# A two-layer decoder trunk on one Trainium2 core: value products moved behind the next round's scores, and the first expert quad's first two weight slots cut by k block

## The reference

```
h = rms_norm(x);  z = h @ w_in + b_in          # 8448 columns: A q/k/v, B u/v, C q/k/v, three gates
A: 16 heads of 64, 4 key/value heads, window 128, learned sinks, partial rotary
B: u * (tril(W_s) @ LN(v) + b), 12 groups of 64 channels, chunks of 128 tokens
C: 12 heads in three groups of 4, (window, dilation) = (128,1), (512,4), (2048,16), groups combined
   by softmax weights
x = x + (sum_i sigmoid(gate_i) * (branch_i @ P_i)) @ w_out
x = x + moe(rms_norm(x))                       # top-1 of 4 groups, top-2 of its 8 experts, SwiGLU
```

## Time and profile before

| what | value |
|---|---|
| runs, median of 3 | 1018.7 us |
| profiled execution | 1018.59 us |
| its span | 1016.9 us |
| PE busy | 951.8 us, 94% |
| DVE busy | 560.8 us, 55% |
| ACT busy | 431.0 us, 42% |
| attention rounds, first layer | about 134 to 246 us |
| attention rounds, second layer | about 636 to 748 us |
| first quad, first layer | about 316 to 336 us |
| first quad, second layer | about 818 to 838 us |
| HBM read | 310.20 MB |

### The profile page before, as it was taken

How to read it: one execution, slowest core, us unless ns; L and a number is a source line. 1 busy time by engine, 2 the same in 40 slices (tenths; PEclk the granted TensorE clock), 3 DMA queues, 4 the chain that set the end, 5 groups by cost and what they waited for, 6 DMA issues and landing times.

```text
span 1016.9 us, 15601 instructions
## 1 busy us (share of the span) xinstructions
PE 951.8 (94%) x5898; PEld 665.8 (65%) x5898; DVE 560.8 (55%) x1328; ACT 431.0 (42%) x920; POOL 58.6 (6%) x74
## 2 busy tenths in 40 slices
PE   9999999999999995976999999999999999977787
PEld 7888877778886441532588888777888954434333
DVE  7666787786883332220276668788868634122212
ACT  5434666766444120210363455666764441111122
POOL 1120400000010000000003004000000100000000
PEclk9999999999999998998999999999999999999989
DMA  9975644248999999999997756342599999999996
GB/s 351 348 244 191 193 138 125 83 123 321 361 391 398 422 426 423 426 427 426 418 392 239 239 180 201 125 125 64 174 355 345 406 418 413 425 425 425 426 427 273
DMA packets 97114, 313.03 MB, mean 308 GB/s; under 512 B 13424, under 2 KB 18576, under 8 KB 74512
## 3 DMA queue, kind: packets, MB, share of 16 engines
q1 hardware_dynamic: 96704, 312.04, 80.3%
q10 hardware_dynamic: 336, 0.02, 0.0%
HBM read 310.20 MB, written 1.84 MB: 307 GB/s over the span
## 4 chain that ended last, share of the span: by engine, by line
PE 76%; DMA 13%; SPq 7%; DVE 2%; ACT 1%; issue 1%; POOL 0%; DVEq 0%; POOLq 0%
PE ps L1488 16%; PE ps L1490 15%; PE ps L1489 15%; SPq L505 7%; PE ps L2154 6%; DMA arena<-in_w_expert_up_dram 5%; DMA arena<-in_w_expert_gate_dram 3%; DMA ring_rest<-in_w_expert_up_dram 3%; DMA ring_rest<-in_w_expert_down_dram 3%; PE ps L2128 2%; PE ps L1611 2%; PE ps L1513 2%; PE ps L2228 2%; PE ps L1623 2%; PE ps L2240 2%; PE ps L2099 1%
## 5 line engine op out<-in xcount | busy, mean ns | idle before, releaser
L1140 DVE TENSOR_TENSOR split_w<-arena,split_w 128x512 fp32r<-128x512 f32 (+1 forms) x352 | 232.9, 700 | 101.1 <-ACT split_w L933 97.6
L1488 PE MATMUL ps<-split_w,split_a 128*128 128x512 f32 (+1 forms) x736 | 283.9, 386 | 0.1
L1490 PE MATMUL ps<-split_w,split_a 128*128 128x512 f32 (+1 forms) x736 | 277.1, 376 | 0.0
L1489 PE MATMUL ps<-split_w,split_a 128*128 128x512 f32 (+1 forms) x736 | 276.7, 376 | 0.0
L933 ACT CAST split_w<-arena 128x1024 fp32r<-128x1024 f32 (+1 forms) x171 | 175.8, 1031 | 176.9 <-PE ps L1490 170.0
L1488 PEld LDWEIGHTS ps<-split_w,split_a 128*128 128x128 f32 x736 | 138.5, 188 | 26.6 <-issue 2.2
L1490 PEld LDWEIGHTS ps<-split_w,split_a 128*128 128x128 f32 x736 | 138.4, 188 | 26.0
L1489 PEld LDWEIGHTS ps<-split_w,split_a 128*128 128x128 f32 x736 | 138.7, 188 | 23.5
L2385 DVE SCALAR_TENSOR_TENSOR acts<-ps,wslot,acts 128x256 f32<-128x256 f32 x16 | 7.7, 483 | 171.6 <-ACT acts L2055 148.5
L2154 PE MATMUL ps<-arena,rows 128*32 128x512 f32 x416 | 90.0, 615 | 9.6 <-DMA arena<-in_w_expert_up_dram 6.9
L2154 PE MATMUL ps<-ring_rest,rows 128*32 128x512 f32 x352 | 76.0, 634 | 12.8 <-DMA arena<-in_w_expert_up_dram 12.8
(11 more groups left out here) (284 smaller groups left out, 1074.6 us busy)
## 6 DMA issues: line engine op xcount, KB each, us to landing
arena<-in_w_in_dram SPq DMA_DIRECT2D x62, 1024.0 KB, 5.3
arena<-in_w_expert_down_dram SPq DMA_DIRECT2D x36, 1024.0 KB, 19.5
arena<-in_w_expert_gate_dram SPq DMA_DIRECT2D x34, 1024.0 KB, 23.9
arena<-in_w_expert_up_dram SPq DMA_DIRECT2D x32, 1024.0 KB, 24.0
ring_rest<-in_w_expert_down_dram SPq DMA_DIRECT2D x24, 1024.0 KB, 17.4
ring_rest<-in_w_expert_gate_dram SPq DMA_DIRECT2D x22, 1024.0 KB, 23.9
ring_rest<-in_w_expert_up_dram SPq DMA_DIRECT2D x22, 1024.0 KB, 25.5
arena<-in_w_proj_a_dram SPq DMA_DIRECT2D x8, 1024.0 KB, 5.1
```

The costliest lines, as they stand in the source:

```text
L1140: dve.tensor_tensor(wlo[:, jj % 2, cols], half_slot(jj, w)[:, cols], whi[:, jj % 2, cols].bitcast(F32), ALU.subtract).then_inc(low_split i ...
L1488: pe.matmul(o, hi, rhs_hi, start=first, stop=False)
L1489: pe.matmul(o, hi, rhs_lo, start=False, stop=False)
L1490: return pe.matmul(o, lo, rhs_hi, start=False, stop=last)
```

## The change

The value products leave `pv(b)`. A new `products_of(b - 1)` stands between `scores(b + 1)` and `pv(b)`, from round 1 on; so the products of rounds 0 to 7, and the common ones of rounds 8 and 9, each come one item and the following scores later. On ACT `o_out` moves with them: `o_out(b - 1)` now stands before `pv_out(b)`. In the first quad, positions 1 and 2 now hold one k block of four experts each, so their loads are made of runs of 1 KB instead of 2 KB, PE raises `gu_part` once more after k block 0, and position 21 waits for k block 0 alone. All other counts of `gu_part` go up by one.

```diff
+        def first_blocks(slot):
+            return slot.rearrange("p (e a n) -> p e a n", e=4, a=2)
...
                 for to, w in enumerate((w_expert_gate, w_expert_up)):
+                    if part == 0:
+                        src = w[l, 0:4].rearrange("e (p k) f -> p e k f", p=P)
+                        sp.dma_start(first_blocks(slot)[:, :, to, :], src[:, :, pair, :]).then_inc(done, 16)
+                        continue
...
-                            sp.wait_ge(before_me.gu_part, 4)
+                            sp.wait_ge(before_me.gu_part, 5)
...
+                            if b >= 1:
+                                o_out(b - 1)
                             pv_out(b)
...
                             if b + 1 < BATCHES:
                                 exps(b + 1)
-                            if b < BATCHES - 1:
-                                o_out(b)
...
                             gates_conv(45 + 2 * b, (lambda: turn_probs(b, 2)) if b >= 8 else None)
+
+                        def products_of(b):
                             if b < 8:
                                 product_pair(b)
                             elif b % 2:
                                 products(b)
...
                                 scores(b + 1)
+                                products_of(b - 1)
                                 pv(b)
...
-                        sp.wait_ge(R.gu_part, FIRST_CHUNKS[i] // 2 + 1)
+                        sp.wait_ge(R.gu_part, FIRST_CHUNKS[i] // 2 + (2 if FIRST_CHUNKS[i] else 1))
...
-                        act.wait_ge(R.gu_part, 4)
+                        act.wait_ge(R.gu_part, 5)
...
-                            w = first_parts(places(FIRST_CHUNKS.index(2 * i + e // 2))[:, 0, :])[:, e % 2, :, (k % 2) * F:(k % 2 + 1) * F]
+                            if i == 0:
+                                w = first_blocks(places(FIRST_CHUNKS.index(k))[:, 0, :])[:, e, :, :]
+                            else:
+                                w = first_parts(places(FIRST_CHUNKS.index(2 * i + e // 2))[:, 0, :])[:, e % 2, :, (k % 2) * F:(k % 2 + 1) * F]
...
+                        if k == 0:
+                            mm.then_inc(R.gu_part, 1)
                     mm.then_inc(R.gu_part if i < 3 else R.gu_ready, 1)
```

## The result

The kernel after took 1020.37 us (median of 20 runs, 1019.37 to 1022.71), the kernel before 1018.5 us beside it (20 runs, 1017.55 to 1020.11). The ratio is 1.0018, 95% interval 1.0012 to 1.0025: slower by 1.9 us. The forecast was 1020.2 us, 1.6 us slower, with "within 0.2%" as the likeliest case. That the kernel got slower is clear of noise; whether by less than 0.2% is not, since the interval reaches past it. The profiled execution of after took 1022.33 us, one of its longest, so its stages are compared, not its total.

What follows compares the result with a forecast made beforehand. PE (busy 951.8 of 1016.9 us) bounds up to the second quad's end, then the full DMA queue. Per layer -0.36 + 0.12 + 0.35 + 0.69 = +0.80 us, so 1018.59 + 1.6 = 1020.2 us; range 1017.0 to 1022.4.

Steps and rivals of the forecast that it cites:

- Even rounds: Rounds 0, 2, 4 and 6, at whose products no chunk ends: -0.09 us each, together -0.36 a layer.
- products behind scores would cost what transposes did: On PE, scores to products costs the same as the change it replaces, so only 0.09 us of item to products goes.
- Rounds 1, 3 and 5: Products there hid DVE's evacuation; the next item waits 0.13 us, less 0.09 saved: +0.04 us each, together +0.12.
- PE sees DVE's end 0.05 us later: Delay from DVE's end to PE's start, read before round 9's transposes (216.12 to 216.17), used for the evacuation waits.
- Rounds 7 and 9: Items 60 and 64 wait for DVE's evacuations in groups of three matmuls: +0.35 us in round 7, +0.69 in round 9.
- ACT: nothing: `o_out` moved before `pv_out` on ACT costs nothing; without the covering item PE would wait up to 0.8 us a round.
- Part two: First quad's 1 KB runs and earlier load of position 21: gap at 321 closes, gap at 346 grows, worth nothing.
- The price at half speed: First quad's 1 KB runs, if moved at half speed, cost 1.9 us a layer after gaps; 1024.0 us in all.
- A: Rival: the fixed 0.15 us goes with the 0.09 in all nine moved products: 1017.5 us; chance 0.1.
- B: Rival: DVE is early enough, no waits at items 48, 52, 56, 60 and 64: 1017.0 us; chance 0.12.
- C: Rival: the earlier load passes to the layer's end, 0.37 us less in each layer: 1019.5 us; chance 0.08.
- D: Rival: scores to products and products to transposes cost 0.1 us each on top: 1023.8 us; chance 0.2.

Runs made afterwards that it cites:

- e2: Kernel before with only the new first quad (1 KB runs, early load of position 21), products in their old place: 1018.55 us against 1019.28, ratio 0.9997.
- e6: As e2, but position 21 waits for both k blocks as in the kernel before: 1018.11 us against 1018.82 for the kernel before, ratio 0.9993.
- e7: Kernel before with only the products of rounds 0, 2, 4 and 6 moved, plus the new first quad: 1017.50 us against 1018.82, ratio 0.9985.
- e3: Kernel before with only the products of rounds 0, 2, 4 and 6 moved, first quad as before: 1017.15 us against 1019.28, ratio 0.9984.
- e4: Kernel before with only the products of rounds 1, 3, 5, 7 and 9 moved, first quad as before: 1022.55 us against 1019.28, ratio 1.0038.
- e5: Kernel after with DVE's `group_max` behind both evacuations and the second low half: 1019.59 us against 1018.82 for the kernel before, ratio 1.0005.

## Why the prediction was right

The mechanism came as forecast, and the total (1020.2 against 1020.37) is better than its terms, which is in part luck. Two errors offset: against the forecast, the even rounds gave 0.24 us a layer more, and the odd ones took 0.27 + 0.09 + 0.07 = 0.43 more. So a layer lost 0.99 to 1.02 us instead of 0.80, and both layers together 2.0 instead of 1.6 (1.9 by the medians). And the forecast started from 1018.59, where the kernel before now has 1018.5. One slip in the range changes nothing: the middle between 1020.2 and 1023.8 is 1022.0, not 1022.4.

**Even rounds: mis-sized.** Forecast -0.09 each, measured -0.15. Besides the 0.09 us of item to products, the way back to full-array work costs 0.05 to 0.06 us, which I had missed in the transposes behind the products (0.16 for the first, 0.11 for the next). Before, a round paid both twice, now once. That products behind scores would cost what transposes did was right (0.86 us). The Trainium skill, TensorEngine Tiling (Array Packing), Key Properties, says that each change of mode drains TensorE; the trace agrees for the changes to and from the full array. For scores to products, a change as well, it shows nothing beyond 0.86.

**Rounds 1, 3 and 5: mechanism right, size off.** Forecast +0.04, measured +0.12 to +0.14. The step that failed is "PE sees DVE's end 0.05 us later", taken from the row before round 9's transposes. At an item's first matmul it is 0.15 us.

**Rounds 7 and 9: right, each a little low.** Forecast +0.35 and +0.69, measured +0.44 and +0.76. PE's start behind the first evacuation is later by the same 0.10 us; that does not add up, because the second evacuation has its own date, met as forecast (PE goes on 0.06 us behind it). What adds is that the matmul behind the second wait takes 0.34 us to the next and not 0.23 (201.51 to 201.85), in item 64 0.22 and not 0.12 (221.24 to 221.46). I had counted that step once per item.

**ACT: nothing, right.** In round 1 its copy waits 0.59 us for the products at 144.57 and ends 0.29 us before `pv_out` can start, and PE has no wait for ACT in the rounds.

**Part two: nothing, right.** The gap at 321 closes and the one behind the second quad's release grows. Both were mis-sized: the single slices gave 0.37 and 0.19 us, but 250 to 380 KB changed places, 0.6 to 0.9 us at 426 GB/s. As it is an exchange, the sum did not suffer. e2 and e6 bound the whole of it to 1.0006 and 1.0001 from above, and with the even rounds alone it makes no difference either (e7 0.9985, e3 0.9984). The price at half speed, 1.9 us a layer, would be 1.0037 and is out.

**The rivals.** A (fixed parts go with the handovers) falls: scores and products start to start are 0.86 + 0.80, as apart; of its 0.15 us more, only 0.06 came, and only in the even rounds; in the others PE waits for DVE anyway. B (no waits) falls by the row of waits and by e4. C (early load passes to the end) has the exchange of gaps against it, and e6, which is no slower without the early load (0.9993) than e2 with it (0.9997). The times alone don't exclude it: by e2's interval up to 0.0013, 1.3 us, stays possible. D (dearer handovers) falls: no handover got dearer.

## What to carry to other kernels

Work that stands between the last matmul into a bank and the first that overwrites it is cover for the evacuation; before it is moved, subtract it from the time in which the other engine evacuates, at every place separately, since the same move can gain at one parity and lose at the other. Group what uses another tiling of the array together, as each excursion from the full array and back costs, here 0.15 us. A transfer started earlier gained nothing here, since a later release still left the queue a gap, and that gap grew.

## What was unexpected of the hardware

The same signal, DVE's end to PE's start, has two sizes here: 0.15 us at the first matmul of an item behind a wait (148.19 to 148.34, 200.53 to 200.68, 220.26 to 220.41), and 0.05 to 0.06 us at a second wait (201.45 to 201.51, 221.18 to 221.24) and before round 9's transposes. In both cases the load of the weights had not gone ahead: it starts at 200.65 and 201.51, with the matmul or 0.03 us before it. What makes the difference was not tried.

A matmul behind a stop inside an item has a longer distance to the next one, as an item's first has anyway (161.99 to 162.32): 0.34 us instead of 0.23 in item 60, 0.22 instead of 0.12 in item 64. In e5, where item 60's second group has no wait, it is 0.23 again. So a second short wait cost 0.10 us more than its idle time at these two places; no run shows the reason.
